# One transformer block on one core: GpSimd's order around the indexer's sums, value weights in buffers of their own, norm sums in PSUM, last block in halves

## What is computed

```python
h = rmsnorm(x, g_pre_mix)
qa, ka, va, qi, ki, wi, qb, kb, vb, gate_a, gate_b = split(h @ w_in)
score[t, s] = sum_h wi[t, h] * 8**-0.5 * relu(qi[t, h] . ki[s] * 64**-0.5)      # the indexer, 8 heads
keep the 128 best admissible s of each t; softmax attention over them with a relative bias -> o_a
stick-breaking attention of qb, kb, vb -> o_b
m = sigmoid(gate_a) * (o_a @ W_a) + sigmoid(gate_b) * (o_b @ W_b)
x = x + rmsnorm(m @ w_out, g_post_mix)
h = rmsnorm(x, g_pre_ffn)
x = x + rmsnorm((silu(h @ w_g) * (h @ w_u)) @ w_down, g_post_ffn)
```

## Time and profile before

| | |
|---|---|
| three runs | 801.53, 796.28, 802.0 us; median 801.53 |
| the profiled execution | 796.3 us, of which 794.5 us lie between first and last instruction |
| mean granted TensorE clock | 0.996 |
| busy | PE 98%, PEld 82%, POOL 53%, DVE 49%, ACT 45% |
| DMA | 79.40 MB, 100 GB/s on average |

### The profile page before, as it was taken

The page is one execution under the profiler, slowest core; times in us unless marked ns, Lnnn a source line. Parts: engine busy times, 40 slices in busy tenths (PEclk is TensorE's granted clock), DMA queues, the critical chain, the costliest instruction groups (busy, mean ns, idle before and its releaser), DMA issues.

```text
span 794.5 us, 10497 instructions
## 1 busy us (share of the span) xinstructions
PE 778.4 (98%) x3700; PEld 650.4 (82%) x3700; DVE 386.1 (49%) x542; ACT 354.5 (45%) x567; POOL 420.0 (53%) x246
## 2 busy tenths in 40 slices
PE   9997999999999999999999999999999999999996
PEld 6776888888888888888888988888888888888885
DVE  5669979999657565389337100000000020444464
ACT  6664266867758585633256222222222232233242
POOL 5566456766777878334563244444444443443463
PEclk9999999999999999999999999999999999999999
DMA  9401342311303231223293113333233332222312
GB/s 341 137 14 54 115 158 87 106 54 54 106 16 113 71 109 54 80 67 118 90 308 106 54 53 106 106 106 92 76 97 106 106 106 89 75 102 106 106 54 106
DMA packets 100011, 79.40 MB, mean 100 GB/s; under 512 B 2817, under 2 KB 90889, under 8 KB 99978
## 3 DMA queue, kind: packets, MB, share of 16 engines
q1 hardware_dynamic: 99978, 78.97, 31.5%
HBM read 76.85 MB, written 3.68 MB: 101 GB/s over the span
## 4 chain that ended last, share of the span: by engine, by line
PE 88%; DVE 6%; DMA 2%; ACT 2%; issue 1%; POOL 0%; SPq 0%; POOLq 0%; DVEq 0%; ACTq 0%
PE ps L469 22%; PE ps L448 18%; PE ps L450 18%; PE ps L449 18%; PE ps L533 3%; PE ps L677 2%; PE ps L666 2%; DMA raw<-in_w_gate_up 1%; PE ps L649 1%; PE ps L651 1%; DVE score L1349 1%; DVE keep_buf L1406 1%; DVE e_buf L1414 1%; DMA raw<-in_w_out 1%; DVE k_both L1357 0%
## 5 line engine op out<-in xcount | busy, mean ns | idle before, releaser
L1118 POOL TENSOR_TENSOR w_lo<-raw,w_hi 128x1024 fp32r<-128x1024 f32 x82 | 197.9, 2415 | 262.3 <-ACT w_hi L787 236.3
L448 PE MATMUL ps<-h_hi,w_hi 128*128 128x512 f32 (+1 forms) x608 | 235.9, 388 | 0.3 <-DVE h_lo L1289 0.3
L450 PE MATMUL ps<-h_hi,w_lo 128*128 128x512 f32 (+1 forms) x608 | 233.9, 385 | 0.0
L449 PE MATMUL ps<-h_lo,w_hi 128*128 128x512 f32 (+1 forms) x608 | 233.8, 384 | 0.0
L787 ACT ACTIVATE w_hi<-raw 128x1024 fp32r<-128x1024 f32 (+1 forms) x78 | 82.6, 1061 | 294.0 <-PE ps L450 195.6
L450 PEld LDWEIGHTS ps<-h_hi,w_lo 128*128 128x128 f32 x608 | 114.3, 188 | 22.6
L448 PEld LDWEIGHTS ps<-h_hi,w_hi 128*128 128x128 f32 x608 | 114.4, 188 | 21.5 <-issue 0.7
L449 PEld LDWEIGHTS ps<-h_lo,w_hi 128*128 128x128 f32 x608 | 114.5, 188 | 21.0
L1559 DVE TENSOR_TENSOR act<-silu,ps 128x512 f32 (+1 forms) x22 | 15.1, 688 | 211.3 <-PE ps L450 211.3
L1200 POOL TENSOR_TENSOR w_lo<-raw,w_hi 128x1024 fp32r<-128x1024 f32 x30 | 77.4, 2584 | 30.6 <-ACT w_hi L907 30.2
L1564 DVE TENSOR_TENSOR d_lo<-act,d_hi 128x512 fp32r<-128x512 f32 x18 | 41.8, 2328 | 52.9 <-ACT d_hi L1066 52.9
(11 more groups left out here) (191 smaller groups left out, 1322.8 us busy)
## 6 DMA issues: line engine op xcount, KB each, us to landing
raw<-in_w_gate_up SPq DMA_DIRECT2D x44, 512.0 KB, 4.6
raw<-in_w_in SPq DMA_DIRECT2D x40, 512.0 KB, 4.2
raw<-in_w_down SPq DMA_DIRECT2D x22, 512.0 KB, 3.8
xf<-in_first SPq DMA_DIRECT2D x8, 512.0 KB, 6.5
raw<-in_w_out SPq DMA_DIRECT2D x8, 512.0 KB, 3.9
x_in<-in_x SPq DMA_DIRECT2D x4, 512.0 KB, 8.4
raw<-in_w_branch_sb SPq DMA_DIRECT2D x8, 256.0 KB, 3.0
raw<-in_w_branch_sparse SPq DMA_DIRECT2D x8, 256.0 KB, 3.0
```

What stands on the lines that cost most here:

```text
L448: mm(acc, whi_c, a_hi_, start=first, stop=False)
L449: mm(acc, whi_c, a_lo_, start=False, stop=False)
L450: return mm(acc, wlo_c, a_hi_, start=False, stop=last)
L1118: nc.gpsimd.tensor_tensor(w_lo[:, at(u), :], raw[:, at((d % 2) * 2 + u), :], w_hi[:, at(u), :], sub).then_inc(w_lo_done, 1)
```

## The change

It has six parts.

1. `rel_in_rows` is loaded earlier and turned within the first pass (bank 7); VectorE makes `rel_t` before the queries' rests. GpSimd then writes `f_bias` right after the subtraction of the first two tiles, before the value weights.
2. The value weights' first four tiles get buffers of their own (`wv_hi`, `wv_lo`). ScalarE rounds tiles 0 and 1 before the queries, 2 and 3 before the relus. GpSimd fills `ends` (memset and four `affine_select`, before on VectorE), subtracts tiles 0 and 1, and then waits until all eight sums are done before anything else.
3. The keys' roundings are done by VectorE, from PSUM, one of them in place of ScalarE's. `w_tok` is computed ahead of the last pair's rests. Head 0 goes to banks 5 to 7 and waits for one pair of rests only, head 1 for all.
4. The first value tile takes its blocks in the order 0, 3, 1, 2. VectorE's `k_rest` of the first two heads moves into the rounds of `best_eight`.
5. Residual sums and scaled results of the first norm stay in PSUM: VectorE scales PSUM to PSUM and adds `x1` there; ScalarE squares it there and copies it to `x1` (a new 128x1024 instruction, four in all), and `turn` waits for that copy.
6. The last block of the down projection is done in halves of 512 columns, each squared by itself; the gain is multiplied before the root is known, and the last two instructions scale and add at once, both on VectorE.

The diff, cut to its core:

```diff
+    def value_slot(c):
+
+        return (wv_hi, wv_lo, c) if c < LAST else (w_hi, w_lo, c % 2)
...
+            if c == 2 + TB:
+                pe.wait_ge(small_in, 16)
+                mm(ps[0:HEADS, 7, 0:BUCKETS], rel_in_rows[:, :], ident[0:BUCKETS, 0:BUCKETS],
+                   start=True, stop=True).then_inc(small_turned, 1)
...
         def indexer_scores(h):
-            j, s = h // 2, h % 2
+            s = (h + 1) % 2
             if h >= 2:
                 pe.wait_ge(idx_relu, h - 1)
             if h == 0:
-                pe.wait_ge(qi_rest_done, PAIRS)
+                pe.wait_ge(qi_rest_done, 1)
                 pe.wait_ge(ki_halves_done, 3)
                 pe.wait_ge(w_tok_done, 1)
-                pe.wait_ge(small_kept, 1)
+            if h == 1:
+                pe.wait_ge(qi_rest_done, PAIRS)
...
         for c in range(KC):
             weights(T_V + c)
-            ins = token_tile(c % 2, h_hi[:, c, :], h_lo[:, c, :], c == 0, c == KC - 1,
+            hi, lo, slot = value_slot(c)
+            ins = token_tile(slot, h_hi[:, c, :], h_lo[:, c, :], c == 0, c == KC - 1,
+                             order=(0, 3, 1, 2) if c == 0 else range(TB),
...
+        split_value(0)
+        split_value(1)
+
         for t in range(PAIRS):
             if t == 2:
                 sc.wait_ge(kw_done, 1)
-                run(ki_hi[0:HD, :], ps[0:HD, 6, :], ACT.Copy).then_inc(ki_hi_done, 1)
-                run(wi_t[HD:KW, :], ps[HD:KW, 6, :], ACT.Copy, scale=float(HEADS) ** -0.5).then_inc(ki_hi_done, 1)
+                run(wi_t[HD:KW, :], ps[HD:KW, 6, :], ACT.Copy, scale=float(HEADS) ** -0.5).then_inc(wi_t_done, 1)
...
         def square_x1(t):
             sc.wait_ge(x1_done, t + 1)
-            square(2, t, x1[:, t, :], y_buf[:, t, :])
+            square(2, t, two_banks(t), y_buf[:, t, :])
+            run(x1[:, t, :], two_banks(t), ACT.Copy).then_inc(x1_kept, 1)
...
+        gp.wait_ge(chunk_done, KC)
+        nc.gpsimd.memset(ends[:, :], 0.0).then_inc(ends_done, 1)
+        split_value(0)
+        split_value(1)
+        gp.wait_ge(ends_done, 1)
+        for b in range(TB):
+            own = PACK[b + 1] + b * P
+            ins = nc.gpsimd.affine_select(ends[:, own:own + P], ends[:, own:own + P], pattern=[[-1, P]], base=0,
+                                          channel_multiplier=1, compare_op=ALU.not_equal, fill=1.0)
+        ins.then_inc(ends_done, 1)
+        gp.wait_ge(idx_summed, HEADS)
...
         def scale_out(t):
-            scale_sum(0, 1, t, g_mix_row)
+            scale_sum(two_banks(t), 1, t, g_mix_row)
 
         def norm_x1(t):
-            scale_rows(2, t, y_buf[:, t, :], x1[:, t, :], g_ffn_row[:, :])
+            scale_rows(2, t, y_buf[:, t, :], two_banks(t), g_ffn_row[:, :])
...
         def sum_x1(t):
             ve.wait_ge(x1_in[t], 16)
-            residual(0, t, x1_done)
+            ve.wait_ge(y_normed, t + 1)
+            tt(two_banks(t), two_banks(t), x1[:, t, :], ALU.add).then_inc(x1_done, 1)
...
+        tt(y_buf[:, t, halves[0]], bank(2 * t), g_out_row[:, halves[0]], ALU.mult).then_inc(y_normed, 1)
...
+        tt(y_buf[:, t, halves[1]], bank(2 * t + 1), g_out_row[:, halves[1]], ALU.mult).then_inc(y_normed, 1)
+        inverse(3, t)
         ve.wait_ge(y_normed, 2 * TB + 1)
-        half = slice(512, D)
-        tt(x1[:, t, half], x1[:, t, half], y_buf[:, t, half], ALU.add).then_inc(y_done[1], 1)
+        for half in halves:
+            stt(x1[:, t, half], y_buf[:, t, half], rstd[:, i:i + 1], x1[:, t, half], ALU.mult, ALU.add).then_inc(y_done[1], 1)
```

More of the change, by code:

```diff
@@ L471, in token_block, with token_tile @@
             return ins
-        def token_tile(slot, act_hi_, act_lo_, first, last, order=range(TB), before=None, signal=None):
+        def token_tile(slot, act_hi_, act_lo_, first, last, order=range(TB), before=None, signal=None,
+                       hi=w_hi, lo=w_lo):
             for i, t in enumerate(order):
@@ L477, in token_tile @@
                     before(i)
-                ins = token_block(t, slot, act_hi_, act_lo_, first, last)
+                ins = token_block(t, slot, act_hi_, act_lo_, first, last, hi, lo)
                 if signal is not None and i < TB - 1:
@@ L481, in token_tile, with block_in_halves, block_by_block @@
             return ins
-        def block_by_block(end, hi, lo, acts, ready, before=None, lead=LAST):
+        def block_in_halves(t, hi, lo, acts):
+            for n in range(2):
+                for i, (a_h, a_l) in enumerate(acts):
+                    for p, (a, w) in enumerate(((a_h, hi), (a_h, lo), (a_l, hi))):
+                        ins = mm(bank(2 * t + n), a[:, t * P:(t + 1) * P], w[:, i, n * 512:(n + 1) * 512],
+                                 start=False, stop=i == LAST - 1 and p == 2)
+                ins.then_inc(tile_done if n else block_done, 1)
+        def block_by_block(end, hi, lo, acts, ready, before=None, lead=LAST, blocks=TB):
             steps = [(t, i) for part in ((0, lead), (lead, LAST)) for t in range(2) for i in range(*part)]
-            for t, i in steps + [(t, i) for t in range(2, TB) for i in range(LAST)]:
+            for t, i in steps + [(t, i) for t in range(2, blocks) for i in range(LAST)]:
                 if t == 0:
@@ L774, in _ @@
         block_by_block(T_END, wd_hi, wd_lo, [(h_hi[:, i, :], h_lo[:, i, :]) for i in range(LAST)],
-                       lambda i: activations(FC - LAST + i), lead=2)
+                       lambda i: activations(FC - LAST + i), lead=2, blocks=TB - 1)
+        block_in_halves(TB - 1, wd_hi, wd_lo, [(h_hi[:, i, :], h_lo[:, i, :]) for i in range(LAST)])
     @block.scalar
@@ L888, in _ @@
         split_qk(1)
-        for c in range(KC - 1):
-            split((T_V + c + 2) // 2, c % 2)
+        for c in range(LAST, KC):
+            split_value(c)
+        split(T_FILL // 2, 0)
         for t in range(TB):
@@ L1191, in _ @@
         split_qk(1, T_V + 2)
-        for c in range(KC):
-            split((T_V + c + 2) // 2, c % 2)
+        for c in range(2, KC):
+            split_value(c)
+        split(T_FILL // 2, 0)
+        split(T_FILL // 2, 1)
         split_v(0)
@@ L1357, in k_rest @@
             tt(k_both[o, h, :], proj[r, 2 * g + 1, :], k_both[r, h, :], sub).then_inc(k_lo_done, 1)
-        k_rest(0)
-        k_rest(1)
-        ve.wait_ge(idx_summed, HEADS)
-        nc.vector.memset(ends[:, :], 0.0).then_inc(ends_done, 1)
-        ve.wait_ge(ends_done, 1)
-        ve.wait_ge(const, 2)
-        for b in range(TB):
-            own = PACK[b + 1] + b * P
-            ins = nc.vector.tensor_copy(ends[:, own:own + P], ident[:, :])
-        ins.then_inc(ends_done, 1)
         ve.wait_ge(idx_summed, HEADS)
@@ L1401, in _ @@
             best_eight(r)
+            if r in (2, 4):
+                k_rest(r // 2 - 1)
         def kept_after(i):
```

137 lines of the change are left out of this document (84 added, 53 removed).

## The result

| | before | after |
|---|---|---|
| median (range) | 800.9 us (796.28 to 802.0, 4 runs) | 788.27 us (787.88 to 789.95, 4 runs) |
| profiled execution, of it span | 796.3, 794.5 | 788.6, 786.8 |
| mean granted TensorE clock | 0.996 | 0.999 |

The ratio is 0.986, with a 95% interval of 0.983 to 0.989: 12.6 us less. I had forecast 795.4 and "within 1%", and the change is faster by more than that. The time lies inside the range. Of the profiled executions I had forecast a difference of 6.1 us; it is 7.7.

The account below looks back on a forecast made before the run. TensorE, busy 98% of the span, was taken as the bound, with time to gain in indexer waits and lower clock. Terms -6.2 + 1.2 - 1.1 = -6.1 us, from the median 801.53, gave 795.4; range 787.5 to 803.

Parts of the forecast that it names:

- within 1%: Whole kernel: the outcome class given the highest chance, 0.59, against faster 0.36 and slower 0.05.
- The start of the sums and the silence: Indexer and value projection: earlier scores and sums, GpSimd silent until the eighth sum; -6.2 us.
- So 1.5 us are lost: Indexer: head 5's scores wait for relu 3, due at 55.7 but ready at 57.2, delaying the value projection to 61.9.
- rival A: Sums: VectorE is not held up by GpSimd; gain there 8.0 us, -7.9 in all, 793.6; chance 0.18.
- The tail: After the last matmul: half-width square, two VectorE instructions replace scaling and addition; -1.1 us (-1.5 to -0.5).
- Sum +1.2: Norms: ScalarE's four copies lengthen the path to `turn`, less VectorE's savings; +1.2 us in all (0 to 3).
- That leaves +0.8 for block 1: Norms, block 1: two copies in a row cost 1.6 us, less a 0.5 DMA wait and VectorE's savings.
- 0.2 saved twice: Norms: VectorE operations with one operand from PSUM, not two from SBUF beside GpSimd, each save 0.2 us.
- I expect the same spread and predict from the median: 795.4.: Whole kernel: the 5.5 us spread between executions stays, so -6.1 us is applied to the median 801.53.
- B: Indexer: the bias row takes 13.3 us beside VectorE's other work too; gain 3.0, -2.9 in all, 798.6; chance 0.12.
- C: Value projection: GpSimd's silence delays the third value tile, sums ending at 75; costs 4.1 us, 805.7; chance 0.05.
- D: Norms: each copy counts in full, 4 x 1.0, plus 2 us of waiting; -1.3 in all, 800.2; chance 0.05.

Follow-up runs that it names:

- bias_last: Kernel after with GpSimd's bias row written after the first two value subtractions, beside the sums; 787.83 us.
- tail_back: Kernel after with the old last block (one square, scaling and addition in four instructions); 790.85 us.
- norm_alone: Kernel before with only the change's norm part (part 5); 798.12 us, ratio 0.998 to the kernel before.
- norm_back: Kernel after with the norm change taken out: residual sums in SBUF again, no ScalarE copy; 790.26 us, repeated at 790.34 us.
- sums_alone: Kernel after with the old norms and the old tail, leaving the indexer and value projection change; 791.34 us.
- splits_in_sums: Kernel after with GpSimd's subtractions of value tiles 2 and 3 put back in the middle of the sums; 794.8 us.
- norm_copy_sbuf: Kernel after with residual sums in SBUF again, but ScalarE's copies kept, from SBUF into an idle buffer; 793.93 us.

## Why the prediction was wrong, and where it was right

**The start of the sums and the silence: right in kind, 1.9 us too small.** The wait for `w_tok` is gone, the chain of a late sum, a late relu and a standing TensorE too, and the clock is 1.00 where I expected it. I put -6.2; the ledger has -8.1. What failed is the step "So 1.5 us are lost", between the first sum and head 5's scores. I had VectorE held to the end of all GpSimd work (52.9) and head 0's 1.3 us after it. In fact the bias row took 9.1 us, not 10.1, VectorE got in as soon as the subtractions were over, ahead of the `affine_select` (1.2 us that I had counted), and all three ended at 52.67 in an execution that had started 1.05 us late. Head 5 was not late. Without the start's 1.05 us the value projection begins at 60.0, not at 61.9. The third value tile waits 0.2, not 0.4. `bias_last` shows rival A's mechanism (VectorE not held at all); by the ledger it gives 0.2 us more.

One reading under this part was wrong, though the forecast doesn't suffer from it. I took the 7.07 us for the hold by the two subtractions, and wrote that the sums keep their pace beside the small bias instructions. But that addition started at 58.93, while a small one ran (58.81 to 59.13) and 1.8 us before the first subtraction (60.74). Five more small ones of 0.33 to 0.38 us passed it, then both subtractions. So in the sums a hold can outlast the running instruction; why it does stays open. The Trainium skill's rule ("SBUF — State Buffer", Who interferes with whom) has whoever is first keep the port for the whole instruction; by it the addition would have been in at 59.13, so the trace does not agree with it in the way that I wrote.

**The tail: right.** -1.37 for -1.1, confirmed by `tail_back`.

**The norms: the wrong sign in the median.** For the execution that I read, "Sum +1.2" is right in sign and twice too large: it is +0.64, of it +0.4 at the `turn` of block 1 ("That leaves +0.8 for block 1"). But over all executions the part gives 1.9 us (`norm_alone` against before) or 2 us (after against `norm_back`). I had the two halves of it at hand: the rule that whoever comes first keeps the other out, and GpSimd's subtractions right beside sums with two SBUF inputs. In the kernel before:

```profile
409.66 1.23 DVE L1516 TENSOR_TENSOR x<-x,y_buf 128x1024 f32<-128x1024 f32 x1
416.24 1.43 DVE L1516 TENSOR_TENSOR x<-x,y_buf 128x1024 f32<-128x1024 f32 x1
...
410.47 6.11 POOL L1118 TENSOR_TENSOR w_lo<-raw,w_hi 128x1024 fp32r<-128x1024 f32 x2 [5.83 <-ACT w_hi L1047]
416.75 6.51 POOL L1247 TENSOR_TENSOR wu_lo<-raw,wu_hi 128x1024 fp32r<-128x1024 f32 x2 [0.16 <-ACT wu_hi L1052]
```

I counted this meeting as "0.2 saved twice", from rows in which VectorE was first. I did not ask what the same rows would read had GpSimd come first, though they are only 0.5 to 0.8 us apart and GpSimd hangs, by way of ScalarE's rounding, on a load. The Trainium skill's rule ("SBUF — State Buffer", Who interferes with whom) states this case, and in the norms the traces agree: 2.9 to 3.4 us where GpSimd came first, 1.23 to 1.51 where it did not. The other rule that I weighed ("VectorE: DVE Perf Modes", Rules for kernel authors) leaves the choice, to accept the pace from PSUM or to copy to SBUF first for many operations; I read it as speaking for the copy. Here that pointed the wrong way: from PSUM the scaling takes 1.28 us and the sum 1.23, no more than from SBUF.

**The median: the step that cost most.** "I expect the same spread and predict from the median: 795.4." This step failed: I treated the 5.5 us between the two kinds of execution as something that every kernel keeps. The runs show in its place a wait in the norms that falls or doesn't by who comes first, 4.1 us in `sums_alone`, and the change takes it away: -12.6 us in the median where the profiled executions differ by 7.7. It isn't the whole spread. `norm_alone` still spreads by 3.65 us, and starts differ by up to 2 us. Of the 12.6 us, `sums_alone` has 8.7 (800.0, the median of all 74 executions of before, less 791.3), `norm_alone` 1.9, the tail's rows 1.4. Together 12.0; the missing 0.6 is within what the medians of before differ by from one set of executions to another (798.5 to 801.7). These shares are rough: the interval of `sums_alone` against the kernel before run beside it is 0.986 to 0.994, 5 to 11 us.

**The rivals.** A (VectorE not held) came nearest, 793.6: its gain of 8.0 is what the ledger has, though VectorE was held for 2 us. But it too took the step to the median as I did. B, C and D didn't happen. That the silence makes the third value tile late is true, at 0.2 us. That waits at the norms could be execution-dependent was in none of them.

One thing is inferred: no profile of a long execution of the kernel before itself was caught. That its long ones are those of `sums_alone` rests on `norm_alone`, which changes nothing but the norms and has none of 12 above 799.7, where the kernel before run beside it had 9 of 17.

## What to carry to other kernels

If executions of one kernel fall into two groups, ask which two engines meet by less than a microsecond in the profile at hand, and read the rows once with the order turned round: the profile may show the lucky case, and the time to be had is not in it. VectorE's two-tile operations on a critical path should take one operand from PSUM while GpSimd subtracts large tiles, or GpSimd's instructions should be cut small; a copy of 1 us on ScalarE's side can be paid by that. That only one tile comes from SBUF is not enough by itself: head 0's `TENSOR_SCALAR` reads `relu_buf` and a column of `w_tok`, writes `score` in SBUF, and its first took 2.38 us in the kernel after and 8.08 in `splits_in_sums`, against 0.49 in `bias_last`. And a gain is forecast from the profiled execution to the profiled execution; what the median does is a term of its own.

## What the runs showed of the hardware that I had not expected

- VectorE's sum with one PSUM operand and one in SBUF, its result in PSUM, started 0.5 us into a GpSimd subtraction: 1.23 us, and no loss for GpSimd (4.75 a pair). With both in SBUF: 2.9 to 3.4 us, or, started first, 1.2 to 1.5 and GpSimd's pair at 6.1 to 6.5 (5.4 to 5.8 where VectorE was held for one of the two).
- In the norms a held operation gets in after one subtraction. In the sums it looked otherwise: 7.07 us in before, over five small instructions and two subtractions, and 8.08 in `splits_in_sums`, over seven instructions. What makes the difference was not tried.
- GpSimd's small bias instructions (8 partitions) and its four `affine_select` did not always hold VectorE: head 0's three took 1.08 us beside the former in `bias_last`, and in the kernel after they ended at 52.67, while the latter ran to 53.06. But five bias instructions passed the waiting addition in before, and the four `affine_select` the waiting multiplication in `splits_in_sums`.
- The first 25 us differ by up to 2 us between executions of one kernel. In the four profiles that started about 2 us late (`sums_alone`, `norm_copy_sbuf`, `tail_back` and one of `norm_back`) the granted clock was 0.66 to 0.69 from 10 to 15 us; in the others it was 1.00.
